# Layer norm of a two-block network: the offset taken by GpSimd, the weight rounding moved, 24 idle products

## The chip, the cores and the metric

The kernel runs as one program on one core of one Trainium2 chip. The metric is device time in microseconds (us), from one launch to its end. The core's engines are named as the profile names them: PE is TensorE (matrix products), DVE is VectorE, ACT is ScalarE, POOL is GpSimd, and SP is SyncE, which here only issues the loads from device memory. SBUF is the on-chip memory that all of them address, and PSUM holds the results of products in eight banks, ps[0] to ps[7].

## What is computed

The reference runs a first network of two layers on 256 tokens of width 1024 and hands its result to a second one of two layers, which puts 16 learned tokens in front (272 tokens). Cut to what matters here, each stage ends in a layer norm:

```python
def _layernorm(t, g, b):                      # first network, once in each of 2 layers
    mu = jnp.mean(tf, axis=-1, keepdims=True)
    var = jnp.mean(jnp.square(tf - mu), axis=-1, keepdims=True)
    return (tf - mu) * lax.rsqrt(var + NORM_EPS) * g + b
...
x = _layernorm(DEEPNORM_ALPHA * x + out, ln_g[layer], ln_b[layer])
...
for l in range(DEPTH):                        # second network, three in each of 2 layers
    h = layer_norm(ALPHA * h + 0.5 * swiglu(h, ffn1_w_up[l], ffn1_w_down[l]), ln_g[l, 0], ln_b[l, 0])
    mix = hybrid_mixer(h, ...)
    h = layer_norm(ALPHA * h + mix, ln_g[l, 1], ln_b[l, 1])
    h = layer_norm(ALPHA * h + 0.5 * swiglu(h, ffn2_w_up[l], ffn2_w_down[l]), ln_g[l, 2], ln_b[l, 2])
```

So there are eight layer norms in a row of stages, and the next stage's large products need the normalised activations of the one before.

## The kernel before

**Layout.** The activations live transposed in SBUF as `xT`: eight tiles (o = 0 to 7) of 128 features by 256 or 272 tokens. Every large product is taken to nearly full precision with three products of a rounded format: an operand is split into a rounded part (`x_hi`, `w_hi`) and the rest (`x_lo`, `w_lo`), and hi*hi, hi*lo and lo*hi are summed in PSUM. Weights come in pieces of 512 KB into `raw`; ACT rounds 128x1024 of them into `w_hi` (`split`, the instruction stands at line 1082), DVE subtracts to get `w_lo` (line 1585). There are four places for such split pieces, used in turn (`p % PARTS`).

**What sets the order.** Nothing is scheduled: each engine has one hand-written instruction stream that it takes strictly in order, and semaphores (`S[...]`) tie the streams together.

**A layer norm before the change.** The last product of a stage ends in tiles o = 6 and 7. PE takes the mean in two steps: most of it is taken off early (`centre`), the rest, the *offset*, is summed by products with a constant into ps[4] (`off_part`, line 639), and the mean square into ps[3] (`square_part`, line 646). Then, on the four engines:

- PE runs 30 idle products (`keep_warm(WARM)`, line 653) whose result nobody reads, and then `first_three`: for each of the eight tiles three products of `x_hi` with `w_hi` (line 612), three of `x_hi` with `w_lo` (line 614), and, once `x_ready` says that `x_lo` is there, three of `x_lo` with `w_hi` (line 617).
- ACT squares the offset out of ps[4] into `off2`, waits for the variance, takes its logarithm and the exponential (together the reciprocal root, `rstd`), then does `last_split()`, the rounding of the fourth piece of weights of the next stage, and then the eight `x_hi` tiles (lines 1132 and 1133), each as soon as DVE has scaled it.
- DVE subtracts `off2` from the mean square (line 1720), takes the offset from `xT` straight out of ps[4] two tiles at a time (`less_offset`, line 1707, four times), scales each tile (`scaled`, line 1710) and makes each `x_lo` (`lower`, line 1715), and at the end the `w_lo` of that fourth piece.
- POOL adds the bias to `xT` when all `x_lo` are made (`add_bias`, line 527), for the next stage's sum; before that it has nothing to do in the norm.

The eighth norm is the last work of the program: `final=True` skips `x_hi` and `x_lo`; DVE scales the eight tiles, ACT adds the bias, PE turns them, and they are stored. There the 30 idle products stand beside DVE's work.

Two kinds of norm differ in what ACT does just ahead. Behind an output projection (norms 1, 2, 4 and 7) DVE sums tile 7 late, and ACT squares it a moment before the offset is complete. Behind a feed-forward stage (norms 3, 5, 6 and 8) tile 7 is squared well before that.

Of the kernel before, what the change touches and what calls it, by code (L numbers as in the profile page):

```python
# [11 lines left out]
ALU = mybir.AluOpType  # L12
# [68 lines left out]


LO_CREDIT = 3
WARM = 30
WARM_MEM, WARM_X, WARM_W = 4, 4, 8


# [73 lines left out]
def build(nc, a):  # L161
    ctx = ExitStack()
    with ctx:
# [93 lines left out]
        class Cut:  # L257
# [4 lines left out]
            def __call__(self, n, w):  # L262
# [86 lines left out]
                 "qk_ready s_done s_max p_ready mix_ready mix_turned mixT_ready pv_done o_squared osum_done "  # L349
                 "o_var o_rsq att_ready dg_tanh cg_tanh cs_done cs_max cp_ready cn_ready "  # L350
                 "cturned cT_ready cpv_done cross_ready "
                 "y_hi_ready y_split branch_part merged_sum merged_hi merged_ready mean_done centred x_summed off_summed sq_summed sq_ready off_done off_squared var_done var_ready rstd_ready ln_scaled bias_ready x_full "
                 "ff_tanh h_hi_ready h_ready down_part mla_weights conv2_made mla_hi lat_squared lsum_done lvar_ready lrs_ready lat_ready "
                 "krot_done kr_ready q_ready s2_done s2_masked s2_max "
                 "lam_dot lam_exp nega_exp angles_ready p2_ready p2_norm p2_turned p2T_ready pv2_done mla_ready x_out out_turned out_copied_act out_copied_dve")
# [163 lines left out]

        @block.gpsimd  # L520
        def _(pool):
            def add_bias(NL, n):
                pool.wait_ge(S["bias_ready"], NL + 1)
                pool.wait_ge(S["x_ready"], NL * KT + KT + KT)
                for o in range(KT):
                    x = xT[:, o, TOK2 - n:TOK2]
                    m = pool.tensor_tensor(x, x, norm_bias[:, o:o + 1].to_broadcast([P, n]), ALU.add)  # L527
                m.then_inc(S["x_full"], 1)

            pool.memset(idle, 0.0).then_inc(S["idle_ready"], 1)  # L530
            pool.wait_ge(params_in, 16 * 4)
            for l in range(DEPTH):
                for h in range(2):
                    pool.drain()
                    pool.tensor_copy(skip[h * 64:(h + 1) * 64, l, :],
                                     skip_all[h * 64:(h + 1) * 64, l, :].rearrange("p (t h) -> p h t", h=2)[:, h, :])
            pool.drain()
            pool.sem_inc(S["skip_ready"], 1)

            with pool.Fori(0, DEPTH) as l:  # L540
                pool.drain()
                pool.memset(cum_rows[2 * SSD_HEADS:P, :].bitcast(F32), 0.0).then_inc(S["rows_cleared"], 1)
                pool.drain()
                pool.memset(y_sum[:, :], 0.0)
                with pool.Fori(0, 4 * GROUPS // 2) as p:
                    for t in range(2):
                        pool.drain()
                        pool.wait_ge(S["y_squared"], l * 16 + p * 2 + t + 1)
                        pool.tensor_tensor(y_sum[:, :], y_sum[:, :], y_sq[:, t, :], ALU.add).then_inc(S["sq_added"], 1)
                add_bias(l, SEQ)  # L550
            with pool.Fori(0, 3 * DEPTH - 2) as n:
                add_bias(n + DEPTH, TOK2)
            add_bias(4 * DEPTH - 2, SEQ)


        @block.tensor
# [520 lines left out]
        def _(act):  # L1077
            def fn(out, in_, f, **kw):
                return act.activation(out, in_, f, **kw)  # L1079
# [39 lines left out]

            def layer_norm(NL, eps, n, last_split, final=False):  # L1120
                c = slice(TOK2 - n, TOK2)
                act.wait_ge(S["off_done"], NL + 1)
                fn(off2[:, 0:n], ps[4][:, 0:n], ACT.Square).then_inc(S["off_squared"], 1)
                act.wait_ge(S["var_ready"], NL + 1)
                fn(rstd_in[:, 0:n], rstd[:, 0:n], ACT.Ln, bias=const[:, K_EPS + eps:K_EPS + eps + 1])
                act.drain()
                fn(rstd[:, 0:n], rstd_in[:, 0:n], ACT.Exp, scale=-0.5).then_inc(S["rstd_ready"], 1)
                if final:
                    return
                last_split()  # L1130
                for o in range(KT):
                    act.wait_ge(S["ln_scaled"], NL * KT + o + 1)
                    fn(x_hi[:, o, c], xT[:, o, c], ACT.Identity, bias=norm_bias[:, o:o + 1]).then_inc(S["x_hi_ready"], 1)
# [427 lines left out]
        def _(v):  # L1561
# [140 lines left out]
            def layer_norm(NL, g_col, b_col, params, n, last_split, final=False):  # L1702
                c = slice(TOK2 - n, TOK2)

                def less_offset(o):
                    t = xT[:, o:o + 2, c]
                    tt(t, t, wide(ps[4][:, 0:n], 2), ALU.subtract)

                def scaled(o):
                    stt(xT[:, o, c], xT[:, o, c], params[:, ds(g_col + o, 1)], rstd[:, 0:n], ALU.mult,  # L1710
                        ALU.mult).then_inc(S["ln_scaled"], 1)

# [5 lines left out]
                v.wait_ge(S["off_squared"], NL + 1)  # L1718
                v.wait_ge(S["var_done"], NL + 1)
                tt(rstd[:, 0:n], ps[3][:, 0:n], off2[:, 0:n], ALU.subtract).then_inc(S["var_ready"], 1)  # L1720
                less_offset(0)
                less_offset(2)
                v.drain()
                v.wait_ge(S["rstd_ready"], NL + 1)
                if final:
                    for o in range(4):
                        scaled(o)
                    less_offset(4)
                    less_offset(6)
                    v.drain()  # L1730
                    for o in range(4, KT):
                        scaled(o)
                    return
                scaled(0)
                scaled(1)
                less_offset(4)
                lower(0)
                scaled(2)
                lower(1)
                scaled(3)  # L1740
                lower(2)
                less_offset(6)
                scaled(4)
                lower(3)
                scaled(5)
                lower(4)
                scaled(6)
                lower(5)
                scaled(7)
                lower(6)  # L1750
                lower(7)
                last_split()
# [472 lines left out]
```

## Time and profile before

| | us |
|---|---|
| Median of three runs | 2431.14 |
| Lowest and highest | 2430.11, 2431.89 |
| The profiled execution's own time | 2431.46 |
| Its span, first to last instruction | 2429.7 |

The profiled execution's span is 1.8 us shorter than its time, which also holds launch and end. PE's granted clock over the span has a mean of 0.995 of full speed. A row of a timeline gives start (us from the span's start), duration (us), engine, line, operation, result <- operands, shape and number of instructions merged; in square brackets stands how long the engine was idle before it and what ended that. Starts of consecutive instructions of one engine can lie a little ahead of the end of the one before, since they overlap in its pipeline.

### The profile page before, as it was taken

Reading aid. Unit: us, or ns where it says so; the run is one execution under the profiler, and the core shown is the slowest. Engines: PE = TensorE matmul, PEld = TensorE weight load, DVE = VectorE, ACT = ScalarE, POOL = GpSimd, SP = SyncE. Lnnn points to the kernel's source line nnn. Section 1 sums busy time; section 2 is a strip of 40 time slices with the busy share of each in tenths; the row PEclk is TensorE's granted clock in tenths of the full one; section 3 lists DMA queues with packets and bytes.
Section 4 is the critical chain, followed back from the end, with each engine's and each line's share of the span. In section 5 each row is a group of like instructions: output and inputs, shape, how many; then the busy total and the mean of one; then the engine's idle time right before and its main releaser. Section 6 shows DMA issues by size and latency. Waiting matters only on the chain.

```text
span 2429.7 us, 48189 instructions
## 1 busy us (share of the span) xinstructions
PE 2386.0 (98%) x18842; PEld 2287.5 (94%) x18842; DVE 1698.6 (70%) x2509; ACT 1347.1 (55%) x2359; POOL 90.1 (4%) x101
## 2 busy tenths in 40 slices
PE   9999999999999999999999999999999999999999
PEld 8899999999899999999999997899999999789998
DVE  6888777776888867786766565676566656667665
ACT  6788655644687855563444455554444445555444
POOL 0000000000100000000100010010001001001000
PEclk8999999999999999999999999999999999999999
DMA  7454555546345355545455554345545554434553
GB/s 217 122 157 139 158 158 163 165 165 198 106 143 153 122 165 164 153 153 191 146 189 169 173 157 118 111 150 173 171 159 173 174 173 150 130 114 153 190 179 116
DMA packets 401047, 380.20 MB, mean 156 GB/s; under 512 B 28223, under 2 KB 397037, under 8 KB 400765
## 3 DMA queue, kind: packets, MB, share of 16 engines
q1 hardware_dynamic: 397821, 373.87, 48.2%
q10 hardware_dynamic: 3072, 4.20, 0.7%
q8 instruction: 106, 1.74, 0.3%
q14 instruction: 48, 0.39, 0.0%
HBM read 372.77 MB, written 1.05 MB: 154 GB/s over the span
## 4 chain that ended last, share of the span: by engine, by line
PE 80%; DVE 11%; ACT 3%; DVEq 3%; issue 1%; DMA 1%; SPq 1%; ACTq 0%
PE ps L583 22%; PE ps L585 21%; PE ps L584 21%; DVE scratch L1807 3%; DVE w_lo L1585 3%; DVEq L1806 2%; PE ps L805 2%; PE ps L836 1%; PE ps L837 1%; PE ps L838 1%; ACT scratch L1082 1%; ACT w_hi L1082 1%; PE ps L653 1%; PE ps L612 1%; PE ps L614 1%
## 5 line engine op out<-in xcount | busy, mean ns | idle before, releaser
L1585 DVE TENSOR_TENSOR w_lo<-raw,w_hi 128x1024 fp32r<-128x1024 f32 x664 | 811.8, 1229 | 422.9 <-ACT w_hi L1082 421.2
L583 PE MATMUL ps<-x_hi,w_hi 128*128 128x256 f32 (+1 forms) x3664 | 1055.7, 288 | 4.6 <-DVE w_lo L1585 1.8
L584 PE MATMUL ps<-x_lo,w_hi 128*128 128x256 f32 (+1 forms) x3664 | 1042.6, 285 | 0.0
L585 PE MATMUL ps<-x_hi,w_lo 128*128 128x256 f32 (+1 forms) x3664 | 1039.8, 284 | 0.0
L1082 ACT ACTIVATE w_hi<-raw 128x1024 fp32r<-128x1024 f32 x664 | 697.8, 1056 | 445.5 <-PE ps L585 372.6
L583 PEld LDWEIGHTS ps<-x_hi,w_hi 128*128 128x128 f32 x3664 | 690.8, 189 | 30.5 <-issue 24.7
L584 PEld LDWEIGHTS ps<-x_lo,w_hi 128*128 128x128 f32 x3664 | 692.1, 189 | 2.0
L585 PEld LDWEIGHTS ps<-x_hi,w_lo 128*128 128x128 f32 x3664 | 693.7, 189 | 0.0
L583 PE MATMUL ps<-big_r,w_hi 128*128 128x272 f32 (+1 forms) x832 | 238.9, 287 | 0.0
L585 PE MATMUL ps<-big_r,w_lo 128*128 128x272 f32 (+1 forms) x832 | 238.2, 286 | 0.0
L1082 ACT ACTIVATE scratch<-ps 128x256 f32<-128x256 f32 (+9 forms) x328 | 122.3, 384 | 152.1 <-PE ps L838 63.8
L584 PE MATMUL ps<-gates_r,w_hi 128*128 128x272 f32 (+1 forms) x704 | 201.3, 286 | 0.0
L584 PE MATMUL ps<-big_r,w_hi 128*128 128x256 f32 (+1 forms) x640 | 181.3, 283 | 0.0
L1079 ACT ACTIVATE scratch<-ps 128x256 f32<-128x256 f32 (+2 forms) x168 | 66.6, 399 | 172.4 <-PE ps L585 155.9
L585 PEld LDWEIGHTS ps<-big_r,w_lo 128*128 128x128 f32 x832 | 156.6, 188 | 0.0
L583 PEld LDWEIGHTS ps<-big_r,w_hi 128*128 128x128 f32 x832 | 156.3, 188 | 0.2
L583 PE MATMUL ps<-scratch_r,w_hi 128*128 128x256 f32 x512 | 144.2, 282 | 2.6 <-DVE scratch L1996 2.6
L585 PE MATMUL ps<-scratch_r,w_lo 128*128 128x256 f32 x512 | 144.6, 283 | 0.0
L584 PEld LDWEIGHTS ps<-gates_r,w_hi 128*128 128x128 f32 x704 | 132.5, 188 | 0.1
L584 PEld LDWEIGHTS ps<-big_r,w_hi 128*128 128x128 f32 x640 | 120.1, 188 | 0.1
L527 POOL TENSOR_TENSOR xT<-xT,norm_bias 128x272 f32<-128x272 f32 (+1 forms) x56 | 51.9, 959 | 1676.7 <-DVE x_lo L1715 1676.7
L1807 DVE SCALAR_TENSOR_TENSOR scratch<-scratch,pa_all 128x256 f32<-128x256 f32 x192 | 93.7, 488 | 25.9 <-ACT scratch L1079 13.7
(301 smaller groups left out, 3050.3 us busy)
## 6 DMA issues: line engine op xcount, KB each, us to landing
raw<-in_w_in SPq DMA_DIRECT2D x184, 512.0 KB, 4.7
raw<-in_ffn_w_up SPq DMA_DIRECT2D x176, 512.0 KB, 4.3
raw<-in_ffn_w_down SPq DMA_DIRECT2D x64, 512.0 KB, 4.2
raw<-in_mix_w_in SPq DMA_DIRECT2D x64, 512.0 KB, 4.5
scratch<-in_w_in SPq DMA_DIRECT2D x40, 512.0 KB, 4.8
raw<-in_w_mem_kv SPq DMA_DIRECT2D x32, 512.0 KB, 4.9
raw<-in_w_br_ssd SPq DMA_DIRECT2D x32, 512.0 KB, 3.8
raw<-in_ffn_w_down SPq DMA_DIRECT2D x32, 384.0 KB, 3.4
```

The source lines that it names most:

```text
L527: m = pool.tensor_tensor(x, x, norm_bias[:, o:o + 1].to_broadcast([P, n]), ALU.add)
L583: mm(out, wh, xh, start=first, stop=False)
L584: mm(out, wh, xl, start=False, stop=False)
L585: return mm(out, wl, xh, start=False, stop=last)
L612: mm(out, w_hi[:, o, j, :], x[0][:, j, :], start=(j == 0), stop=False)
L614: mm(out, w_lo[:, o, j, :], x[0][:, j, :], start=False, stop=False)
L805: m = mm(b[e * 64:(e + 1) * 64, q], x_dt[:, 2 * d + t, j * 64:(j + 1) * 64], decay[:, j % 4, w], start=(n == 0), stop=(n == 3), skip_group ...
L1079: return act.activation(out, in_, f, **kw)
L1082: return act.activation(out, in_, ACT.Copy, scale=scale)
L1585: tt(w_lo[:, p % PARTS, :, :], raw_at(slot_of(Q, p))[:, :, (p % 2) * P:(p % 2 + 1) * P], wh_f[:, p % PARTS, :, :], ALU.subtract).then_inc( ...
L1806: v.drain()
L1807: m = stt(c, conv_in[:, j, n:n + SEQ], tap(n), c, ALU.mult, ALU.add)
```

## The change

Three things change in every norm.

1. **The offset.** ACT copies it from ps[4] to SBUF (`off_sum`, whose earlier content is used up by then), behind its square, and signals `off_copied`. DVE takes it from tiles 0 and 1 only, with one instruction that now reads `off_sum`. POOL takes it from tiles 2 to 7, one instruction each, and signals `less_off`. DVE's scaling of tile o (2 and up) waits for that signal, and DVE now goes strictly in turn: `lower` of tile o-2, `scaled` of tile o.
2. **The rounding.** `last_split()` of ACT moves from behind the exponential to ahead of the offset's square. DVE's half of it stays at the end.
3. **The idle products.** 24 in place of 30.

```diff
-WARM = 30
+WARM = 24
...
         def _(pool):
+            def less_offset(NL, n):
+                pool.wait_ge(S["off_copied"], NL + 1)
+                for o in range(2, KT):
+                    x = xT[:, o, TOK2 - n:TOK2]
+                    pool.tensor_tensor(x, x, off_sum[:, 0:n], ALU.subtract).then_inc(S["less_off"], 1)
+
             def add_bias(NL, n):
+                less_offset(NL, n)
...
             add_bias(4 * DEPTH - 2, SEQ)
+            less_offset(4 * DEPTH - 1, SEQ)
...
             def layer_norm(NL, eps, n, last_split, final=False):
                 c = slice(TOK2 - n, TOK2)
+                if not final:
+                    last_split()
                 act.wait_ge(S["off_done"], NL + 1)
                 fn(off2[:, 0:n], ps[4][:, 0:n], ACT.Square).then_inc(S["off_squared"], 1)
+                copy(off_sum[:, 0:n], ps[4][:, 0:n]).then_inc(S["off_copied"], 1)
...
-                last_split()
                 for o in range(KT):
...
-                def less_offset(o):
-                    t = xT[:, o:o + 2, c]
-                    tt(t, t, wide(ps[4][:, 0:n], 2), ALU.subtract)
-
                 def scaled(o):
+                    if o >= 2:
+                        v.wait_ge(S["less_off"], NL * 6 + o - 1)
...
-                less_offset(0)
-                less_offset(2)
+                v.wait_ge(S["off_copied"], NL + 1)
+                tt(xT[:, 0:2, c], xT[:, 0:2, c], wide(off_sum[:, 0:n], 2), ALU.subtract)
                 v.drain()
                 v.wait_ge(S["rstd_ready"], NL + 1)
...
```

On DVE, in the third norm (behind the first feed-forward stage, 272 tokens), this stands in a row before, from the variance on; `pc_all` holds the norm's scales and biases, `scratch` here `rstd`:

```order
L1720 TENSOR_TENSOR scratch<-ps,scratch 128x272 [waits var_done,off_squared]
L1707 TENSOR_TENSOR xT<-xT,ps 128x544 x2
L1710 SCALAR_TENSOR_TENSOR xT<-xT,pc_all,scratch 128x272 [waits rstd_ready]
L1710 SCALAR_TENSOR_TENSOR xT<-xT,pc_all,scratch 128x272
L1707 TENSOR_TENSOR xT<-xT,ps 128x544
L1715 SCALAR_TENSOR_TENSOR x_lo<-xT,pc_all,x_hi 128x272 [waits x_hi_ready]
```

and now, at the same place:

```order
L1728 TENSOR_TENSOR scratch<-ps,scratch 128x272 [waits var_done,off_squared]
L1730 TENSOR_TENSOR xT<-xT,scratch 128x544 [waits off_copied]
L1718 SCALAR_TENSOR_TENSOR xT<-xT,pc_all,scratch 128x272 [waits rstd_ready]
L1718 SCALAR_TENSOR_TENSOR xT<-xT,pc_all,scratch 128x272
L1723 SCALAR_TENSOR_TENSOR x_lo<-xT,pc_all,x_hi 128x272 [waits x_hi_ready]
L1718 SCALAR_TENSOR_TENSOR xT<-xT,pc_all,scratch 128x272 [waits less_off]
```

The subtractions out of PSUM are gone, one out of SBUF has come, and each scaling from tile 2 on has a wait for POOL.

On POOL, in the norms of the second network, this stands ahead of the bias now; before, the two rows on `norm_bias` were all:

```order
L526 TENSOR_TENSOR xT<-xT,scratch 128x272 [waits off_copied]
L526 TENSOR_TENSOR xT<-xT,scratch 128x272 x5
L534 TENSOR_TENSOR xT<-xT,norm_bias 128x272 [waits x_ready]
L534 TENSOR_TENSOR xT<-xT,norm_bias 128x272 x7
```

Six instructions that read `xT` and the copied offset (`scratch`) from SBUF stand between the copy and the bias.

On ACT, at the third norm, this stands in a row before, from the last square on:

```order
L1079 ACTIVATE scratch<-xT 128x272 [waits bank_free1]
L1079 ACTIVATE scratch<-ps 128x272 [waits off_done]
L1079 ACTIVATE scratch<-scratch,const 128x272 [waits var_ready]
L1079 ACTIVATE scratch<-scratch 128x272
L1082 ACTIVATE w_hi<-raw 128x1024
L1079 ACTIVATE x_hi<-xT,norm_bias 128x272 [waits ln_scaled] x8
```

and now:

```order
L1087 ACTIVATE scratch<-xT 128x272 [waits bank_free1]
L1090 ACTIVATE w_hi<-raw 128x1024
L1087 ACTIVATE scratch<-ps 128x272 [waits off_done]
L1090 ACTIVATE scratch<-ps 128x272
L1087 ACTIVATE scratch<-scratch,const 128x272 [waits var_ready]
L1087 ACTIVATE scratch<-scratch 128x272
L1087 ACTIVATE x_hi<-xT,norm_bias 128x272 [waits ln_scaled] x8
```

The rounding has moved up past three instructions, and a copy out of PSUM (line 1090, `scratch<-ps`) stands ahead of the logarithm.

## Rows read from the trace of the kernel before

**Rows 1.** The page: busy time by engine, and the chain that ended last.

```profile
PE 2386.0 (98%) x18842; PEld 2287.5 (94%) x18842; DVE 1698.6 (70%) x2509; ACT 1347.1 (55%) x2359; POOL 90.1 (4%) x101
PE 80%; DVE 11%; ACT 3%; DVEq 3%; issue 1%; DMA 1%; SPq 1%; ACTq 0%
```

**Rows 2.** Timeline of PE, third norm: idle products, first and last real products.

```profile
1403.74 3.96 PE L653 MATMUL ps<-mem_hi 128*128 128x256 f32 x30
1407.54 0.54 PE L612 MATMUL ps<-x_hi,w_hi 128*128 128x272 f32 x3
...
1416.18 0.55 PE L617 MATMUL ps<-x_lo,w_hi 128*128 128x272 f32 x3
```

**Rows 3.** Timeline of ACT, third norm: offset's square, logarithm, exponential, rounding.

```profile
1403.68 0.40 ACT L1079 ACTIVATE scratch<-ps 128x272 f32<-128x272 f32 x1 [1.39 <-PE ps L639]
1404.68 0.53 ACT L1079 ACTIVATE scratch<-scratch,const 128x272 f32<-128x272 f32 x1 [0.61 <-DVE scratch L1720]
1405.28 0.43 ACT L1079 ACTIVATE scratch<-scratch 128x272 f32<-128x272 f32 x1
1405.62 1.04 ACT L1082 ACTIVATE w_hi<-raw 128x1024 fp32r<-128x1024 f32 x1
```

**Rows 4.** Timeline of DVE, third norm: variance, offset, scaling, first `x_lo`.

```profile
1404.21 0.44 DVE L1720 TENSOR_TENSOR scratch<-ps,scratch 128x272 f32<-128x272 f32 x1 [2.38 <-PE ps L646]
1404.57 0.71 DVE L1707 TENSOR_TENSOR xT<-xT,ps 128x544 f32<-128x544 f32 x1
...
1405.99 0.50 DVE L1710 SCALAR_TENSOR_TENSOR xT<-xT,pc_all,scratch 128x272 f32<-128x272 f32 x1
...
1407.46 0.49 DVE L1715 SCALAR_TENSOR_TENSOR x_lo<-xT,pc_all,x_hi 128x272 fp32r<-128x272 f32 x1
```

**Rows 5.** Timelines of ACT and PE, first norm: last squares, offset's square, first real product.

```profile
606.79 0.42 ACT L1079 ACTIVATE scratch<-xT 128x256 f32<-128x256 f32 x1 [1.21 <-DVE xT L1668]
607.55 0.38 ACT L1079 ACTIVATE scratch<-ps 128x256 f32<-128x256 f32 x1 [0.34 <-PE ps L639]
...
611.38 0.52 PE L612 MATMUL ps<-x_hi,w_hi 128*128 128x256 f32 x3
```

**Rows 6.** Timelines of DVE and POOL, first layer: POOL beside a weight rounding, and alone.

```profile
81.64 1.23 DVE L1585 TENSOR_TENSOR w_lo<-scratch,w_hi 128x1024 fp32r<-128x1024 f32 x1 [0.30 <-ACT w_hi L1082]
81.99 1.47 POOL L549 TENSOR_TENSOR y_sum<-y_sum,y_sq 128x256 f32<-128x256 f32 x1 [54.42 <-ACT y_sq L1079]
...
96.58 0.73 POOL L549 TENSOR_TENSOR y_sum<-y_sum,y_sq 128x256 f32<-128x256 f32 x1 [3.17 <-ACT y_sq L1079]
96.71 0.89 DVE L1861 SCALAR_TENSOR_TENSOR big<-scratch 128x256 f32<-128x256 f32 x1
```

**Rows 7.** Timelines of DVE and POOL, bias additions beside two-input DVE work.

```profile
621.51 0.79 POOL L527 TENSOR_TENSOR xT<-xT,norm_bias 128x256 f32<-128x256 f32 x1
621.91 0.68 DVE L1807 SCALAR_TENSOR_TENSOR scratch<-scratch,pa_all 128x256 f32<-128x256 f32 x1
...
1419.85 1.66 DVE L1585 TENSOR_TENSOR w_lo<-raw,w_hi 128x1024 fp32r<-128x1024 f32 x1
1420.38 1.61 POOL L527 TENSOR_TENSOR xT<-xT,norm_bias 128x272 f32<-128x272 f32 x1
```

**Rows 8.** Timelines of POOL and DVE, bias additions beside DVE work out of PSUM.

```profile
1211.06 0.61 POOL L527 TENSOR_TENSOR xT<-xT,norm_bias 128x256 f32<-128x256 f32 x1
1211.27 0.43 DVE L2025 SCALAR_TENSOR_TENSOR scratch<-scratch,ps 128x272 f32<-128x272 f32 x1
```

**Rows 9.** Timeline of DVE, eighth norm: the two runs of four scalings.

```profile
2419.48 1.67 DVE L1710 SCALAR_TENSOR_TENSOR xT<-xT,pc_all,scratch 128x256 f32<-128x256 f32 x4
...
2422.42 1.67 DVE L1710 SCALAR_TENSOR_TENSOR xT<-xT,pc_all,scratch 128x256 f32<-128x256 f32 x4
```

**Rows 10.** Windows: stretch, its length, busy time (instructions) of each engine, granted PE clock, DMA.

```profile
125.00:135.00 10.00, 8.90 (x77) 8.05 (x76) 9.68 (x17) 9.37 (x22) 0.00 (x0) 1.00 0.54 169
655.00:660.00 5.00, 3.78 (x18) 3.35 (x16) 4.44 (x10) 4.70 (x12) 0.00 (x0) 0.66 0.43 150
```

More of the change, by code:

```diff
@@ L351, in build @@
                  "cturned cT_ready cpv_done cross_ready "
-                 "y_hi_ready y_split branch_part merged_sum merged_hi merged_ready mean_done centred x_summed off_summed sq_summed sq_ready off_done off_squared var_done var_ready rstd_ready ln_scaled bias_ready x_full "
+                 "y_hi_ready y_split branch_part merged_sum merged_hi merged_ready mean_done centred x_summed off_summed sq_summed sq_ready off_done off_copied less_off off_squared var_done var_ready rstd_ready ln_scaled bias_ready x_full "
                  "ff_tanh h_hi_ready h_ready down_part mla_weights conv2_made mla_hi lat_squared lsum_done lvar_ready lrs_ready lat_ready "
@@ L1725, in layer_norm @@
                 if final:
[L1726 to L1731, printed above, removed]
+                    for o in range(KT):
                         scaled(o)
@@ L1735, in layer_norm @@
                 scaled(1)
[L1736 to L1749, printed above, removed]
+                for o in range(2, KT):
+                    lower(o - 2)
+                    scaled(o)
                 lower(6)
```

## The prediction

> **What bounds the kernel now.** I read the page first. PE is busy for 98% of the span, and 80% of the chain that ended last is PE [rows 1], so what delays PE's real products costs time and what DVE, ACT or POOL spend beside them costs none. PE's "busy" holds idle products, though, so I then read the timelines of the four engines through one norm of each kind. In the third norm [rows 2] 30 idle products start at 1403.74 and the first real one at 1407.54: 0.127 us each. PE never waits in this norm: the eight tiles run from 1407.54 to the last group of three at 1416.18, which is 7 2/3 tiles, 1.13 us each (1.065 with 256 tokens). Within a tile `x_lo` is wanted two thirds in, 0.75 us behind its start. What the idle products cover is the chain ACT square 1403.68, DVE variance 1404.21, ACT logarithm 1404.68 and exponential, done at 1405.71 [rows 3, 4], then scaling and `x_hi`.
>
> **The idle products.** Six fewer: 6 x 0.127 = 0.76 us in each of the seven norms that PE leaves at once, 5.3 us if `x_hi` and `x_lo` are there. In the eighth they stand beside DVE's work and are worth nothing.
>
> **The rounding.** It takes 1.04 us on ACT [rows 3]. Behind a feed-forward stage ACT is idle 1.39 us ahead of the offset's square [rows 3]: it fits and costs nothing. Behind a projection ACT is idle only 0.34 us there, since the last square ends at 606.79 + 0.42 = 607.21 [rows 5]. The rounding then ends at about 608.15, the offset's square starts 0.55 late, at 608.1, and as the variance now waits for it in place of PE's last product (it started 0.53 behind the square's start, now 0.43), the chain is 0.45 us late. DVE's half of the split stays last on DVE and only gets its input earlier; SP's loads hang on that half, not on ACT's.
>
> **The copy.** About 0.35 us on ACT, behind the square and ahead of the logarithm, where ACT is idle 0.61 us [rows 3]: hidden. It is what releases POOL and DVE, at about 1404.4 in the third norm.
>
> **DVE and POOL.** DVE loses three subtractions out of PSUM (about 0.63 us each at their spacing, 0.71 in the row [rows 4]), POOL gets six. The question is what the two do to one another. POOL's form of instruction with two full SBUF operands exists already: alone it takes 0.73 us, but beside a DVE instruction with two SBUF inputs 1.47 us, and it ends 83.46 - 82.87 = 0.59 us behind DVE's end [rows 6]. The other way round, DVE's 256-wide instruction behind a POOL one ends 97.60 - 97.31 = 0.29 us behind POOL's end and takes 0.89 us [rows 6]. When both have a queue of such work they take turns, one each: the POOL addition and the DVE one at 621.5 and 621.9 are stretched to 0.79 and 0.68 us, and at 1419.85 DVE waits behind POOL and at 1420.38 POOL behind DVE [rows 7]. A DVE instruction whose second input is in PSUM (the form that goes) runs beside POOL with neither stretched, 0.43 and 0.61 us [rows 8]. All of DVE's new sequence (the subtraction from the copy, `scaled`, `lower`) has two SBUF inputs, and POOL reads SBUF. So while POOL works, a DVE instruction and a POOL one together take 0.29 + 0.59 = 0.88 us (0.93 with 272 tokens: 0.31 + 0.62), where DVE alone has one each 0.40 (four in 1.67 [rows 9]) or 0.41. The double-width subtraction behind POOL is 0.59: POOL's addition before 1420.38 ends some 0.04 behind that start, at 1420.42, and DVE's 1024 elements at 1419.85 + 1.66 = 1421.51 [rows 7]; these 1.09 us and the 0.29 for 256 elements give about 1 ns an element.
>
> The Trainium skill, "SBUF — State Buffer", "Who interferes with whom", says that a VectorE instruction with two SBUF inputs and a GpSimd one that reads SBUF exclude one another for the whole instruction. The trace agrees on who excludes whom. Read to the letter, a blocked POOL instruction would then need its full 0.73 us, where this trace shows 0.59; by that the sum below would be some 5 us more, 2444, and I go by the row.
>
> **Third norm, step by step (feed-forward kind, 272 tokens).** POOL starts at about 1404.5, just ahead of DVE's place at 1404.57 [rows 4], and holds till 1405.25. Then in turn: subtraction 1405.84, tile 3 off POOL 1406.46, `scaled` 0 1406.77, POOL 1407.39, `scaled` 1 1407.70, POOL 1408.32, `lower` 0 1408.63, POOL 1409.25, `scaled` 2 1409.56, POOL's last 1410.18, `lower` 1 1410.49, and from there 0.41 each: `lower` 2 at 1411.31. `x_hi` 0 is there 0.57 us behind its scaling, 1407.34. PE has ended its idle products at 1406.78 and starts at 1407.40, 0.14 ahead of before; it wants `x_lo` 0 at 1408.15 and gets it at 1408.67 (0.52 late), wants `x_lo` 1 at 1409.80 and gets it at 1410.53 (0.73 late), and finds `x_lo` 2 in time. Sum: -0.14 + 0.52 + 0.73 = 1.1 us later than before. If DVE gets in first, all is 0.56 earlier at the start, and POOL's last turn falls ahead of `lower` 2: -0.68 + 0.50 + 0.73 + 0.21 = 0.75.
>
> **First norm (projection kind, 256 tokens).** Variance 608.53, the subtraction first (608.87 against 608.93 for POOL, near a tie), done 609.55; POOL 610.14; exponential 610.03; `scaled` 0 610.43, `scaled` 1 611.31, `lower` 0 612.19, `scaled` 2 613.07, `lower` 1 613.95, `scaled` 3 614.83, `lower` 2 615.23. PE starts at 611.03 in place of 611.38 [rows 5], then waits 0.49, 0.70 and 0.22: -0.35 + 1.41 = 1.05 us later; with 272 columns a product's slower pace hides up to 0.2 of it. I take 1.0. If POOL gets in first, 1.4.
>
> **Eighth norm.** From the copy on, some 1.43 us ahead of the first scaling of before at 2419.48 [rows 9]: 0.73 + 0.55 + 5 x 0.59 + 5 x 0.29 + 3 x 0.40 = 6.9 us, so the last scaling ends at 2424.95 in place of 2422.42 + 1.67 = 2424.09: 0.8 us later, all of it at the end of the program.
>
> **The sum.** 4 x 1.0 + 3 x 1.1 + 0.8 = 8.1 us. From the profiled execution, 2431.46, that is 2439.6; it lies 0.3 above the median, so 2439.2 for the median. Bounds: DVE first everywhere 4.0 + 3 x 0.75 + 0.75 = 7.0; POOL first everywhere 5.6 + 3.3 + 0.8 = 9.7. Behind the first norm the later bias additions meet one more of DVE's convolution taps: 0 to 0.3. What follows the norms was paced by PE and stays so, thus nothing is won back.
>
> **Rivals.**
> - *No exclusion in this form* (POOL 0.73 each at 0.69 spacing, DVE at its own pace). Then `x_hi` 0 sets the start: 0.35 gained in four norms, 0.74 in three, and in the eighth DVE runs eight scalings in one go, 1.5 less: 5.1 us, 2426. For it: the new sequence is shorter for DVE. Against: rows 6 and 7 show the exclusion for each form.
> - *DVE keeps the way while its queue is full*, since its instructions overlap by 0.08 us, and POOL gets in only where DVE waits (for the exponential, for `x_hi`). The first tiles then come in time, and tiles 4 to 7 wait for POOL, where PE has over 1 us in hand. Gain and loss in a norm are within 0.3 us of one another: 2430 to 2434. Against: at 1420.38 POOL gets its turn between two DVE instructions that were both queued [rows 7].
> - *The clock falls* in PE's new gaps. From 655 to 660, with PE busy 3.78 of 5 us, the granted clock is 0.66, so 1.7 us of PE are lost [rows 10]; once in each of four to seven norms makes 2446 to 2451. Against: from 125 to 135 PE is idle 1.1 us and the clock stays at 1.00 [rows 10], and the new gaps (0.5, 0.7) lie a tile apart with full-rate products between.
>
> **How the numbers follow.** What a measurement can tell here is about 0.2%, 4.9 us: below 2426.3 is faster, above 2436.0 slower. Turn taking, 2437.5 to 2441.5: 0.66. DVE keeps the way: 0.14. No exclusion or nearly none: 0.11. Clock, or longer POOL holds: 0.09. The no-exclusion case lies at the border of faster, so faster 0.10, same 0.15, slower 0.75. The range takes in turn taking with its bounds and the second rival: 2430 to 2442.
>
> **What would show it.** In the changed profile: POOL's six subtractions at 0.8 to 0.95 us spacing, DVE's first scalings 0.88 or more apart in place of 0.40; PE with idle time ahead of its `x_lo` products of tiles 0 and 1 (about 0.5 and 0.7) and none from tile 3 on; in the first norm the offset's square at 0.55 us behind its place relative to PE's last products, in the third none. A mean spacing of POOL near 0.69 with DVE at 0.40 would make the whole sum wrong; PE waiting at tiles 5 to 7 instead would speak for the second rival; a granted clock under 1.00 in a norm for the third.

## The result and the profile after

| | before | after |
|---|---|---|
| Median, us (six runs each) | 2430.62 | 2440.46 |
| Lowest and highest | 2429.33, 2431.89 | 2439.31, 2442.27 |
| Span of the profiled execution | 2429.7 | 2437.5 |

The change makes the kernel slower: ratio 1.004, 95% interval 1.0029 to 1.005, 9.8 us by the medians. The profiled execution is the fastest of its six (2439.31 us). Further on, the kernel without POOL's subtractions and the one with the reciprocal root in PSUM each had one slow execution among ten (5909.26 and 4649.48 us), which their medians include and their ratios leave out.

The page of after, busy time by engine and the chain that ended last, answers to [rows 1]:

```profile
PE 2387.5 (98%) x18794; PEld 2283.4 (94%) x18794; DVE 1707.3 (70%) x2485; ACT 1351.4 (55%) x2367; POOL 134.4 (6%) x149
PE 76%; DVE 13%; ACT 4%; DVEq 3%; issue 1%; DMA 1%; SPq 1%; ACTq 0%
```

POOL's busy time is up by 44.3 us, DVE's by 8.7 although it has 24 instructions less: it is stretched, not loaded. PE's share of the chain falls from 80 to 76%, DVE's and ACT's rise. The view of PE's waits (line, waited for, us in total, times, longest) names where they enter the chain:

```profile
PE ps L620 <- ACT x_hi L1087: 4.7, 7, 0.9
PE ps L625 <- DVE x_lo L1723: 4.1, 12, 0.5
```

Line 620 is the `x_hi` product (612 before), line 625 the `x_lo` product (617 before). Neither was in PE's waits before.

**Third norm after**, behind a feed-forward stage. The timelines of POOL and of DVE answer to [rows 4]:

```profile
1405.07 0.77 POOL L526 TENSOR_TENSOR xT<-xT,scratch 128x272 f32<-128x272 f32 x1 [188.94 <-ACT scratch L1090]
1405.80 1.26 POOL L526 TENSOR_TENSOR xT<-xT,scratch 128x272 f32<-128x272 f32 x1
1407.01 0.96 POOL L526 TENSOR_TENSOR xT<-xT,scratch 128x272 f32<-128x272 f32 x1
...
1409.80 0.97 POOL L526 TENSOR_TENSOR xT<-xT,scratch 128x272 f32<-128x272 f32 x1
```

```profile
1405.19 1.23 DVE L1730 TENSOR_TENSOR xT<-xT,scratch 128x544 f32<-128x544 f32 x1
1406.50 0.85 DVE L1718 SCALAR_TENSOR_TENSOR xT<-xT,pc_all,scratch 128x272 f32<-128x272 f32 x1
1407.27 1.00 DVE L1718 SCALAR_TENSOR_TENSOR xT<-xT,pc_all,scratch 128x272 f32<-128x272 f32 x1
1408.19 1.02 DVE L1723 SCALAR_TENSOR_TENSOR x_lo<-xT,pc_all,x_hi 128x272 fp32r<-128x272 f32 x1
...
1410.98 0.49 DVE L1718 SCALAR_TENSOR_TENSOR xT<-xT,pc_all,scratch 128x272 f32<-128x272 f32 x1
```

The two queues take strict turns: from its third on, POOL starts an instruction every 0.93 us, DVE's scalings and `lower` last 0.85 to 1.02 us in place of 0.49 and 0.50, and at 1410.98, when POOL's six are over, DVE is back at 0.49. PE's timeline of the same stretch, to be read against [rows 2], shows what it pays:

```profile
1408.05 0.62 PE L620 MATMUL ps<-x_hi,w_hi 128*128 128x272 f32 x3 [0.45 <-ACT x_hi L1087]
1408.51 0.54 PE L622 MATMUL ps<-x_hi,w_lo 128*128 128x272 f32 x3
1409.27 0.65 PE L625 MATMUL ps<-x_lo,w_hi 128*128 128x272 f32 x3 [0.22 <-DVE x_lo L1723]
1409.75 0.54 PE L620 MATMUL ps<-x_hi,w_hi 128*128 128x272 f32 x3
...
1411.11 0.64 PE L625 MATMUL ps<-x_lo,w_hi 128*128 128x272 f32 x3 [0.46 <-DVE x_lo L1723]
1411.60 0.54 PE L620 MATMUL ps<-x_hi,w_hi 128*128 128x272 f32 x3
```

The idle time in brackets is only part of it; by starts, the `x_lo` products of tile 0 begin 1.22 us behind the first real product (0.75 is their own pace), those of tile 1 1.36 us behind their tile's start. From tile 2 on there is no wait. The rows show one cost more: a group of three products that PE had to wait for is followed by the next group 0.46 to 0.49 us later (1408.05 to 1408.51, 1409.27 to 1409.75, 1411.11 to 1411.60), where a group without a wait takes 0.37 or 0.38.

**First norm after**, behind a projection: ACT first, then DVE and POOL, to be read against [rows 5]:

```profile
605.58 0.42 ACT L1087 ACTIVATE scratch<-xT 128x256 f32<-128x256 f32 x1 [1.21 <-DVE xT L1678]
605.90 1.04 ACT L1090 ACTIVATE w_hi<-raw 128x1024 fp32r<-128x1024 f32 x1
606.85 0.36 ACT L1087 ACTIVATE scratch<-ps 128x256 f32<-128x256 f32 x1
607.11 0.38 ACT L1090 ACTIVATE scratch<-ps 128x256 f32<-128x256 f32 x1
```

```profile
607.57 0.74 POOL L526 TENSOR_TENSOR xT<-xT,scratch 128x256 f32<-128x256 f32 x1 [337.28 <-ACT scratch L1090]
607.59 1.27 DVE L1730 TENSOR_TENSOR xT<-xT,scratch 128x512 f32<-128x512 f32 x1
```

The offset's square starts 1.27 us behind the last square in place of 0.76: the moved rounding stands between. And POOL has the copy 0.02 us ahead of DVE, whose subtraction then lasts 1.27 us. PE's first real product shows the effect:

```profile
610.42 0.60 PE L620 MATMUL ps<-x_hi,w_hi 128*128 128x256 f32 x3 [0.82 <-ACT x_hi L1087]
```

It starts 4.02 us behind the first idle product (606.40), where before it was 3.77 (611.38 and 607.61). In the third norm POOL is ahead of DVE by 0.12 us (1405.07 and 1405.19). POOL comes first in all eight norms: by 0.02 us behind a projection, by 0.11 or 0.12 behind a feed-forward stage.

**Where the time is.** For each profiled execution I took the distance from the first idle product to the last group of three products of tile 7, and for the eighth norm that from the first product of the means to the end of the span. Against before, in us:

| norm | 1 | 2 | 3 | 4 | 5 | 6 | 7 | 8 and end | sum |
|---|---|---|---|---|---|---|---|---|---|
| kind | proj. | proj. | ffn | proj. | ffn | ffn | proj. | ffn | |
| after | +1.42 | +1.33 | +1.19 | +1.60 | +1.17 | +1.19 | +1.42 | +0.72 | +10.0 |

(Norm 3, for instance: 1417.99 - 1404.36 = 13.63 in place of 1416.18 - 1403.74 = 12.44.) The eighth column uses spans printed to 0.1 us and is no finer than that. Norm 4 is the only one behind a projection in which DVE and POOL work on 272 tokens. This ledger is steadier than the whole time, because in the traces the first norm's first product lies anywhere between 603.1 and 607.5 us, whatever the kernel. The experiments are read with both.

### The profile page after: what moved, and what is told of

Read it like the earlier page. It is cut to its first block, busy times and chain, and to the rows that moved or that the text cites. A ratio compares the mean times of both kernels' runs of the same rounds, so it can differ in the third digit from the quotient of the medians.

```text
span 2437.5 us, 48124 instructions
## 1 busy us (share of the span) xinstructions
PE 2387.5 (98%) x18794; PEld 2283.4 (94%) x18794; DVE 1707.3 (70%) x2485; ACT 1351.4 (55%) x2367; POOL 134.4 (6%) x149
## 4 chain that ended last, share of the span: by engine, by line
PE 76%; DVE 13%; ACT 4%; DVEq 3%; issue 1%; DMA 1%; SPq 1%; ACTq 0%
PE ps L591 21%; PE ps L593 21%; PE ps L592 21%; DVE scratch L1799 4%; DVE w_lo L1595 3%; DVEq L1798 2%; PE ps L813 2%; ACT w_hi L1090 1%; PE ps L844 1%; PE ps L845 1%; PE ps L846 1%; ACT scratch L1090 1%; DVE xT L1718 1%; DMA raw<-in_ffn_w_up 1%; PE ps L862 1%
## 5 line engine op out<-in xcount | busy, mean ns | idle before, releaser
L1090 ACT ACTIVATE scratch<-ps 128x256 f32<-128x256 f32 (+8 forms) x336 | 125.7, 385 | 148.3 <-PE ps L846 63.6
L526 POOL TENSOR_TENSOR xT<-xT,scratch 128x256 f32<-128x256 f32 (+1 forms) x48 | 44.3, 955 | 1791.7 <-ACT scratch L1090 1791.7
```

The lines of the kernel that those rows point to most:

```text
L526: pool.tensor_tensor(x, x, off_sum[:, 0:n], ALU.subtract).then_inc(S["less_off"], 1)
L1090: return act.activation(out, in_, ACT.Copy, scale=scale)
```

## The experiments

Medians of before are those of the runs made beside each experiment on the same chip. Differences are against that median. The ledger of all kernels is at the end of this section.

**POOL's six subtractions taken out.** Is it POOL beside DVE, or the longer chain? This kernel leaves the offset in tiles 2 to 7, so it is a probe of time alone.

```diff
             def add_bias(NL, n):
-                less_offset(NL, n)
...
-            less_offset(4 * DEPTH - 1, SEQ)
...
                 def scaled(o):
-                    if o >= 2:
-                        v.wait_ge(S["less_off"], NL * 6 + o - 1)
```

> The changed kernel without POOL's six subtractions and without DVE's waits for them; the offset stays in tiles 2 to 7, so that part of the norm is left out. All else is as changed: early rounding, copy, DVE's new order, 24 idle products. Theory (POOL and DVE take turns, and that alone costs the time): POOL's bias additions apart, nothing stands beside DVE in the norm, x_hi of tile 0 sets PE's start, 0.35 us ahead of before in four norms and 0.74 in three, and the end 1.5 us ahead: about 5 us less than before, 2425.5, some 15 us less than changed. Rival (the longer chain through the copy, DVE's strict turn or the late square are what costs): stays above 2434.

Measured: 2427.29 us, before 2431.78, ratio 0.9981 (0.9971 to 0.9991), 4.5 us less than before. The timeline of DVE in its third norm:

```profile
1407.30 0.71 DVE L1726 TENSOR_TENSOR xT<-xT,scratch 128x544 f32<-128x544 f32 x1
1408.48 0.92 DVE L1714 SCALAR_TENSOR_TENSOR xT<-xT,pc_all,scratch 128x272 f32<-128x272 f32 x2 [0.46 <-ACT scratch L1085]
1409.57 0.50 DVE L1719 SCALAR_TENSOR_TENSOR x_lo<-xT,pc_all,x_hi 128x272 fp32r<-128x272 f32 x1 [0.17 <-ACT x_hi L1085]
```

The same instructions, with their operands in SBUF as in the changed kernel, take 0.71 us for the subtraction, 0.92 for two scalings together and 0.50 for the `lower` when POOL is silent (changed: 1.23, 1.77 and 1.02). So these operands cost nothing by themselves, and the whole loss, some 14 us between this kernel and the changed one, comes with POOL's six instructions. The rival (chain, order, late square) falls as the main cause. The ledger's gain, 3.9, is less than the 5.1 expected: 0.16 to 0.21 behind a projection in place of 0.35, and 0.50 to 0.52 behind a feed-forward stage in place of 0.74.

**30 idle products again in the changed kernel.**

```diff
-WARM = 24
+WARM = 30
```

> The changed kernel with 30 idle products again. Theory: in the changed kernel PE already waits 0.45 to 0.88 us for x_hi of tile 0 behind its 24 products, so six more (0.76 us) fill that wait in four norms and delay the start by 0.3 in three, most of which the wait for x_lo of tile 0 takes up: within 1 us of the changed kernel, 2440 to 2441.5. Rival (the gaps that the missing idle products leave cost PE something, by clock or otherwise): 3 us or more faster than changed. A second rival (the cut is worth its 5.3 us in any setting): 2445.

Measured: 2439.52 us, before 2431.78, ratio 1.0035 (1.0022 to 1.0047). That interval and that of the changed kernel overlap for the most part, and norm by norm the two are within 0.04 us of one another. Its third norm starts the real products 0.11 us later and ends 0.03 us later. So the cut of six products is worth at most 0.3 us in the changed kernel's ledger, and the gaps it leaves cost nothing that the runs can tell.

**24 idle products alone.** The kernel before with `WARM = 24`.

> The kernel before with 24 idle products and nothing else. Theory: x_hi of tile 0 is there about 0.45 us ahead of PE's start in every norm, x_lo of tile 0 0.3 to 0.45: gain 4 x 0.44 + 3 x 0.30 = 2.7 us, 2428. Rival (the idle products cover the chain exactly): no change. Rival (each of the 42 removed products counts): 5.3 us less, 2425.3.

Measured: 2430.6 us, before 2431.78, ratio 0.9993 (0.9984 to 1.0003): no difference that the runs can tell. The ledger has -0.29 to -0.31 in norms 1, 2 and 7 and -0.17 to -0.19 in norms 3 to 6, 1.6 together, where I expected 2.7. PE's timeline, third norm, and ACT's:

```profile
1406.44 0.61 PE L612 MATMUL ps<-x_hi,w_hi 128*128 128x272 f32 x3 [0.24 <-ACT x_hi L1079]
```

```profile
1404.85 1.04 ACT L1082 ACTIVATE w_hi<-raw 128x1024 fp32r<-128x1024 f32 x1
1405.79 0.92 ACT L1079 ACTIVATE x_hi<-xT,norm_bias 128x272 fp32r<-128x272 f32 x2
```

`x_hi` of tile 0 ends at about 1406.3, and PE starts on it at once, 3.47 us behind its first idle product; before it was 3.80. So the start comes 0.33 us sooner here, and 0.31 to 0.38 in the seven norms. Some 0.08 is lost again because the first group now stands behind a wait, and in norms 3 to 6 as much again in tile 0's `x_lo` group, which stretches in the same way (0.45 in place of 0.38). The idle products were within half a microsecond of what they had to cover.

**POOL's part alone**: the changed division of the offset, with `last_split()` back behind the exponential and 30 idle products.

> The changed division of the offset (copy, POOL's six, DVE's one) with the rounding back behind the exponential and 30 idle products. Theory: turn taking costs about 0.85 us in each of the four norms behind a projection (there the chain is no longer 0.45 late), 1.2 in the three behind a feed-forward stage and 0.75 at the end: about 7.8 us above before, 2438.4, so 2 us less than the changed kernel. Rival (the early rounding costs nothing or gains): 2440 or more, equal to or above the changed kernel.

Measured: 2437.61 us, before 2431.78, ratio 1.0028 (1.0018 to 1.0039), 5.8 us more than before. The ledger has +0.87 to +0.98 in three of the norms behind a projection (+1.21 in norm 4), +1.20 behind a feed-forward stage, +0.74 at the end, 8.4 in all, against 7.8 expected. It is 1.7 less than the changed kernel's ledger, all of it behind projections. The moved rounding costs 0.4 to 0.5 us there once the chain is bare.

**The moved rounding alone** (30 idle products, no POOL):

```diff
             def layer_norm(NL, eps, n, last_split, final=False):
+                if not final:
+                    last_split()
                 act.wait_ge(S["off_done"], NL + 1)
...
-                last_split()
```

> The kernel before with the moved rounding alone, 30 idle products. Theory: behind a projection the chain is 0.45 us late, but x_hi of tile 0 (611.0) and x_lo of tile 0 (612.05) still come just ahead of PE's wish (611.4 and 612.1): no change, within 1 us of before. Rival (the rounding costs by itself): 1.8 us or more above before.

Measured: 2432.41 us, before 2430.97, ratio 1.0005 (0.9996 to 1.0015). Ledger: 0.0 behind feed-forward, +0.05 to +0.14 behind projections. As forecast, with 30 idle products the late chain is all but hidden; the median is 1.4 us above before, which the interval doesn't tell from nothing.

**Both, 24 products and the moved rounding, on the kernel before.**

> The kernel before with the moved rounding and 24 idle products. Theory: behind a feed-forward stage as with 24 products alone (0.17 us less each), behind a projection the late chain takes the gain back: together 0.5 to 1 us less than before, about 1 us more than with 24 products alone. Rival (the moved rounding frees ACT and lets the cut pay): 3 us less than before.

Measured: 2433.09 us, before 2430.97, ratio 1.001 (1.0001 to 1.002). The ledger says -0.2 in all (-0.16 to -0.20 behind feed-forward, +0.04 to +0.14 behind projections). Norm by norm that is the expected pattern, but its sum is below the 0.5 to 1 us of gain expected, and the whole time is 2.1 us above before, clear of zero by its interval. That is a miss which the norms don't explain: 0.3 of it is in the last column of the table below, and the rest is open. PE's timeline in the first norm shows the late chain where the cut should have paid (PE waits 0.51 us for `x_hi`):

```profile
610.61 0.59 PE L612 MATMUL ps<-x_hi,w_hi 128*128 128x256 f32 x3 [0.51 <-ACT x_hi L1079]
```

**DVE's subtraction out of PSUM again, everything else changed.** In the changed kernel POOL came first. What is that worth?

```diff
-                tt(xT[:, 0:2, c], xT[:, 0:2, c], wide(off_sum[:, 0:n], 2), ALU.subtract)
+                tt(xT[:, 0:2, c], xT[:, 0:2, c], wide(ps[4][:, 0:n], 2), ALU.subtract)
```

> The changed kernel, with DVE's one subtraction (tiles 0 and 1) read out of ps[4] in place of the copy; rstd stays in SBUF. In the changed kernel's trace POOL comes first in every norm and DVE's subtraction lasts 1.27 us behind it in place of 0.68. Theory (who comes first at the copy is worth one POOL hold, 0.6 us a norm): the subtraction runs beside POOL, all that follows on DVE is 0.5 us earlier, and each norm is 0.4 us shorter: about 3 us less than changed, 2437. Rival (the start does not matter, the turns behind it set the end): within 1 us of changed.

Measured: 2438.42 us, before 2431.37, ratio 1.0027 (1.0018 to 1.0037), 7.05 above before. The ledger has 6.4 in place of 10.0: 0.42 to 0.48 less in each norm. DVE's timeline, third norm:

```profile
1405.21 0.71 DVE L1730 TENSOR_TENSOR xT<-xT,ps 128x544 f32<-128x544 f32 x1
1406.38 1.44 DVE L1718 SCALAR_TENSOR_TENSOR xT<-xT,pc_all,scratch 128x272 f32<-128x272 f32 x2 [0.46 <-ACT scratch L1087]
```

The subtraction keeps its 0.71 us beside POOL, and POOL's second instruction beside it keeps 0.77 in place of 1.26. The scalings, which still read `rstd` from SBUF, are still stretched: two take 1.44 us, where they took 1.77 in the changed kernel and 0.92 without POOL. For the subtraction, the place of one operand decides. This experiment takes the subtraction out of the collision; it doesn't put DVE first in it, and no run does that.

**The reciprocal root in PSUM too.** With DVE's subtraction out of PSUM as in the experiment above, the scalings can be freed in the same way if it is the second SBUF operand that counts: ACT writes the exponential into ps[3], whose mean square DVE has read by then.

```diff
-                fn(rstd[:, 0:n], rstd_in[:, 0:n], ACT.Exp, scale=-0.5).then_inc(S["rstd_ready"], 1)
+                fn(ps[3][:, 0:n], rstd_in[:, 0:n], ACT.Exp, scale=-0.5).then_inc(S["rstd_ready"], 1)
...
-                    stt(xT[:, o, c], xT[:, o, c], params[:, ds(g_col + o, 1)], rstd[:, 0:n], ALU.mult,
+                    stt(xT[:, o, c], xT[:, o, c], params[:, ds(g_col + o, 1)], ps[3][:, 0:n], ALU.mult,
```

> The changed kernel, with the reciprocal root written by ACT into ps[3] in place of SBUF, and DVE's one subtraction (tiles 0 and 1) read out of ps[4] again: scaled and the subtraction then have one SBUF input each, only lower keeps two. POOL's six subtractions stay. Theory (it is the second SBUF input that makes DVE and POOL take turns): DVE's scalings at 0.40 us spacing beside POOL, POOL at about 0.70, one collision at the first lower; about 0.55 us less than before in three norms, 0.15 in four, 1.3 at the end: 3.6 us less than before, 2427.5, some 12 us less than changed. Rival (any DVE work on the same tile, or POOL's own pace, is what delays): within 3 us of the changed kernel.

Measured: 2428.1 us, before 2430.97, ratio 0.999 (0.998 to 1.0), 12 us under the changed kernel with the same six instructions on POOL. Ledger: -0.43 behind feed-forward, -0.11 to 0.0 behind projections, -1.41 at the end, -2.9 in all, against 3.6 expected. Semaphores and order are those of the changed kernel, and only the places of two operands differ, so the scalings' waits for POOL were not what cost the time.

**And the rounding where ACT is idle behind a projection**: between the squares of tiles 6 and 7.

```diff
                 root_table()
-                for o in (6, 7):
-                    square(LH + D_H, o, SEQ)
-                layer_norm(l, 0, SEQ, lambda: split(L + D_Q, KT + 3))
+                square(LH + D_H, 6, SEQ)
+                split_after(L + D_Q, LH + D_H, 7, KT + 3)
+                square(LH + D_H, 7, SEQ)
+                layer_norm(l, 0, SEQ, None)
...
```

The second network has the same edit, and `layer_norm` takes no rounding where it is handed none.

> The kernel of the run before this one, and behind a projection the rounding stands between the squares of tiles 6 and 7, waiting for PE's tile 7, where ACT was idle 1.2 us. Theory (the moved rounding makes the chain 0.45 us late in the four norms behind a projection): offset's square back at its old place, 0.5 us less in each of four norms: 2 us less than the run before, 2425.5, 5.5 us less than the kernel before. Rival (ACT is not late there, or PE does not feel it): equal to the run before.

Measured: 2428.03 us, before 2430.97, ratio 0.9985 (0.9976 to 0.9995): 2.9 us under the kernel before and 12.4 under the changed one by medians, where 5.5 and some 15 were expected. By whole time it is not to be told from the run before it (2428.1). The ledger has -0.41 to -0.58 in every norm and -1.43 at the end, 4.8 in all, 1.9 more than the run before it, as forecast for the norms; the median did not follow. DVE and POOL in its third norm:

```profile
1411.01 0.91 DVE L1720 SCALAR_TENSOR_TENSOR xT<-xT,pc_all,ps 128x272 f32<-128x272 f32 x2 [0.43 <-ACT ps L1087]
1412.10 0.91 DVE L1725 SCALAR_TENSOR_TENSOR x_lo<-xT,pc_all,x_hi 128x272 fp32r<-128x272 f32 x1 [0.18 <-ACT x_hi L1087]
1412.93 0.48 DVE L1720 SCALAR_TENSOR_TENSOR xT<-xT,pc_all,ps 128x272 f32<-128x272 f32 x1
1413.34 0.59 DVE L1725 SCALAR_TENSOR_TENSOR x_lo<-xT,pc_all,x_hi 128x272 fp32r<-128x272 f32 x1
```

```profile
1411.20 0.78 POOL L526 TENSOR_TENSOR xT<-xT,scratch 128x272 f32<-128x272 f32 x1
1411.94 0.77 POOL L526 TENSOR_TENSOR xT<-xT,scratch 128x272 f32<-128x272 f32 x1
1412.67 0.96 POOL L526 TENSOR_TENSOR xT<-xT,scratch 128x272 f32<-128x272 f32 x1
```

While POOL is at work, two scalings with `ps` as their last operand take 0.91 us together, as when DVE is alone, and POOL goes on every 0.73. The first `lower`, which still has two SBUF operands, takes 0.91 by itself: it waits for POOL. Then POOL's next one, at 1412.67, is stretched to 0.96 in its turn.

**The same idle products and rounding, the offset left to DVE.** This is the version above without POOL's part, with `rstd` in SBUF: the kernel before with `WARM = 24` and the roundings placed as above.

> The kernel before with 24 idle products, the rounding moved (behind a projection to between the squares of tiles 6 and 7), and the offset all on DVE out of PSUM as before. Beside the version with rstd in PSUM it lacks POOL's part alone. Theory: DVE's three more subtractions keep x_lo of tile 0 where it was, so PE gains 0.2 us behind a feed-forward stage and 0.3 behind a projection, nothing at the end: 1.7 us less than before, about 2429, and POOL's part is worth 2.3 us once it doesn't collide. Rival (POOL's part is worth nothing even then): equal to the version with rstd in PSUM, 3 us or more under before.

Measured: 2430.74 us, before 2431.37, ratio 0.9998 (0.9988 to 1.0008). Ledger -1.65: -0.17 to -0.19 behind feed-forward, -0.28 to -0.35 in three projection norms (-0.16 in norm 4), nothing at the end. So POOL's part, once it doesn't collide, is worth 3.1 us in the ledger, half of it in the last norm, and some 2.3 in the medians against before (the two intervals overlap a little). The comparison holds the place of `rstd` too, which is in PSUM in the one and in SBUF in the other.

The ledger of all (us against before, "2nd" the extra time between the first product of the means and the idle products of norm 2, which is not in the sum):

| kernel | 1 | 2 | 3 | 4 | 5 | 6 | 7 | 8 | sum | 2nd |
|---|---|---|---|---|---|---|---|---|---|---|
| changed | 1.42 | 1.33 | 1.19 | 1.60 | 1.17 | 1.19 | 1.42 | 0.72 | 10.0 | 0.3 |
| changed, 30 | 1.46 | 1.35 | 1.20 | 1.62 | 1.20 | 1.22 | 1.45 | 0.76 | 10.3 | 0.0 |
| changed, DVE from PSUM | 0.98 | 0.88 | 0.72 | 1.14 | 0.71 | 0.73 | 0.97 | 0.26 | 6.4 | 1.0 |
| POOL's part alone | 0.98 | 0.87 | 1.20 | 1.21 | 1.20 | 1.20 | 0.96 | 0.74 | 8.4 | 0.1 |
| rounding alone | 0.08 | 0.05 | 0.00 | 0.14 | -0.01 | 0.01 | 0.09 | -0.01 | 0.4 | 0.1 |
| rounding, 24 | 0.09 | 0.04 | -0.17 | 0.14 | -0.20 | -0.16 | 0.09 | -0.04 | -0.2 | 0.3 |
| 24 alone | -0.29 | -0.31 | -0.17 | -0.17 | -0.18 | -0.19 | -0.30 | -0.01 | -1.6 | 1.0 |
| 24, rounding placed | -0.28 | -0.35 | -0.17 | -0.16 | -0.19 | -0.17 | -0.30 | -0.03 | -1.7 | 0.4 |
| changed, no POOL | -0.16 | -0.21 | -0.52 | -0.18 | -0.52 | -0.50 | -0.20 | -1.58 | -3.9 | 0.8 |
| changed, rstd in PSUM | -0.05 | -0.11 | -0.42 | 0.00 | -0.43 | -0.43 | -0.05 | -1.41 | -2.9 | 1.1 |
| the same, rounding placed | -0.54 | -0.58 | -0.42 | -0.41 | -0.44 | -0.42 | -0.54 | -1.43 | -4.8 | 1.2 |

The last column is a loss outside the norms' own work. In the timelines the second of the last roundings of the second layer's projection waits for its weights: ACT, with rstd in PSUM,

```profile
1190.58 1.06 ACT L1090 ACTIVATE w_hi<-raw 128x1024 fp32r<-128x1024 f32 x1 [2.43 <-DMA raw<-in_ffn_w_up]
```

and 1.28 us in the kernel before. The squares stand behind it on ACT, the sum of squares on DVE behind those, and PE behind that. The extra time is 0.8 to 1.2 us in five kernels (the 24 products alone, the changed kernel without POOL, rstd in PSUM, the same with the rounding placed, DVE from PSUM), 0.3 to 0.4 in three and 0.0 to 0.1 in the other three. It takes back part of what the better versions gain in their norms; why that load lands later is open, and so is the rest of the difference between ledger and median.

## Why the prediction was right

**Direction, size and range** held: 2439.2 forecast, 2440.46 measured, within 2430 to 2442. The mechanism held as well: VectorE and GpSimd take turns, and that delays `x_hi` and `x_lo` of the first tiles. The size was short: 8.1 forecast, 10.0 by the ledger, 9.8 by the medians. Both lie even above 9.7, my bound for POOL first everywhere, and the whole time came nearer (1.3 us) because the base that I took, 2431.14, lies 0.5 above the median of six runs.

**The idle products.** The 5.3 us "if `x_hi` and `x_lo` are there" never came in full: 0.3 at most in the changed kernel, by putting them back. The condition was stated, and the step-by-step working already let `x_hi` and `x_lo` set the pace. In the experiment on 24 alone I expected 2.7 us and the ledger has 1.6: PE started 0.31 to 0.38 us sooner, where I expected a gain of 0.44 or 0.30 a norm, but a group behind a wait cost 0.08 more, twice in four of the norms.

**The rounding.** Free behind feed-forward (0.00 to 0.01 measured), and forecast 0.45 late behind projections: the square starts 1.27 behind the last one in place of 0.76, so 0.51 late, and its price with the chain bare is 0.4 to 0.5 us a norm.

**Taking turns.** The lap from [rows 6] and [rows 7] was 0.93 us with 272 tokens; POOL's starts are 0.93 apart (1407.01 to 1409.80 holds three laps). With 256 tokens it was 0.88 and is 0.87 (DVE's starts at 610.53, 611.40 and 612.27 in the first norm). The Trainium skill's rule on whole instructions ("SBUF — State Buffer", "Who interferes with whom"), read to the letter, would have made this lap 0.14 longer (POOL's 0.73 in place of 0.59; an estimate); the trace has it that the blocked one needs less than its full time behind the other, and the row was the better guide. PE's waits fell where they were forecast, ahead of `x_hi` of tile 0 and of `x_lo` of tiles 0 and 1, and none from tile 2 on. In the third norm I had 0.52 and 0.73 for the latter two; by starts they are 1.22 - 0.75 = 0.47 and 1.36 - 0.75 = 0.61. The start itself: 0.14 ahead of before forecast, 0.11 ahead measured (from the first product of the means: 6.24 in place of 6.35). Those terms alone give 0.97. The other 0.22 is what the two groups behind a wait for `x_lo` take longer to hand over (0.48 and 0.49 in place of 0.37), which my sum put at nothing. Norm 3 together: 1.1 forecast, 1.19 measured. That it came so near is in part luck, since waits that were too long by 0.17 stood in for the missing term.

**The mis-sized term** is the projection kind: 4 x 1.0 forecast, 1.42, 1.33, 1.60 and 1.42 measured, 5.8 in place of 4.0. The step that failed is "the subtraction first (608.87 against 608.93 for POOL, near a tie)". I had put ACT's copy 0.35 us behind the square; it starts 0.26 behind and POOL gets in 0.02 ahead of DVE. So PE's start in the first norm is 0.25 us later than before, where I had it 0.35 earlier. The bound that I gave for POOL first, 1.4, is what came, but again by terms that offset one another: the waits for `x_lo` were 0.40 and 0.58 (0.49 and 0.70 forecast), and the two groups behind them took 0.10 more each. The experiment with DVE's subtraction out of PSUM starts PE 0.45 sooner in this norm and leaves the waits as they are, so being held behind POOL at the start is worth 0.44 to 0.46 a norm of this kind. It is worth the same behind a feed-forward stage, where I had POOL first from the start.

**The eighth norm**: 0.8 forecast (the step's own times give 0.86), 0.7 measured.

**The rivals.** *No exclusion* gave 2426 and asked for POOL at 0.69 spacing with DVE at 0.40: it is 0.93 and 0.93. The kernel without POOL came out at 4.5 us under before by medians and 3.9 by the ledger, where I had worked out 5.1 for this case. So the condition of that rival didn't hold, and its gain was put too high by 1.2 in the norms. *DVE keeps the way*: no, POOL gets every second turn although DVE's instructions overlap. *The clock*: the stretch from the second norm to near the end has a granted clock of 1.00 in after (columns as in [rows 10]), and so has that from 600 to 620 around the first norm:

```profile
1190.00:2410.00 1220.00, 1199.86 (x9254) 1146.88 (x9253) 787.37 (x1143) 591.88 (x953) 79.28 (x84) 1.00 0.49 156
```

**How close it could have been:** the ledger's 10.0 and the median's 9.8 agree, but for the other kernels the two differ by up to 2.6 us either way (8.4 against 5.8 for POOL's part alone, -0.2 against +2.1 for rounding with 24). The kernel with the rounding placed shows it: its profiled execution is the slowest of its ten (2432.98 us), and its norms are shorter all the same. The part ahead of the first norm and the second layer's stage vary from one profiled execution to the next, so the close agreement for the changed kernel is not to be counted on, and nor is a forecast of the whole time to better than that.

## What to carry to other kernels

Work given to GpSimd that reads SBUF was not free for VectorE here: each VectorE instruction with two SBUF operands took a lap of 0.87 to 0.93 us beside it, in place of 0.40 or 0.41. Count such a lap for each pair, and look in the trace for one GpSimd row beside such work and one alone before moving anything. Where one of VectorE's operands could live in PSUM, the two ran side by side; here moving two of them (the subtraction's and `rstd`) was worth 12 us together. And a cut of filler products pays only up to the first real operand's arrival: read that slack (here 0.31 to 0.38 us, of which 0.17 to 0.3 reached the end of the norm) before cutting six of 0.127.

## What the runs showed of the hardware that was not expected

The place of one operand was enough to end the exclusion, with the instruction otherwise the same: two scalings take 1.77 us beside POOL with `rstd` in SBUF and 0.91 with it in PSUM, and the same subtraction 1.23 and 0.71. While both had such work, the turns were one and one, also between back-to-back DVE instructions whose starts overlap their predecessors by 0.08 us. PE pays more for a wait than the wait: the group of three behind it hands over some 0.1 us later than one without. And who is first at a shared release was settled by 0.02 us in the norms behind a projection (607.57 and 607.59); not being held there was worth 0.44 us in the first norm. A near tie in a forecast is to be priced at both ends.
